# Rotary scores of the cached streams: one fp32r pass over 96 rows in place of an fp32 product over 128

## The chip, the cores and the metric

The kernel runs on one core of a Trainium2 chip. The metric is the device time of one execution in microseconds (us), as the median of several runs. In the views of the profile, PE is TensorE (matrix products and transposes, with PEld for its weight loads), DVE is VectorE, ACT is ScalarE, POOL is GpSimd and SP is SyncE, which here only issues DMAs. TensorE writes into PSUM, the accumulator memory; the others read it from there into SBUF, the working memory of 128 partitions.

## The reference

Two trunk layers of a streaming encoder run on a prompt (512 frames) and on 8 streams of 16 new frames, each stream with 512 cached frames. A layer is a feed-forward block, a block of mixers side by side (latent attention "MLA" with 8 heads, mLSTM, HGRN2), and a second feed-forward block. The change touches the latent attention of the streams:

```python
s = einsum('bqhc,bkc->bhqk', q_lat, ckv) + einsum('bqhr,bkr->bhqk', q_pe, kpe)   # 128 latent + 32 rotary
s = s.astype(float32) * MLA_SCALE                       # streams: every key is allowed
p = softmax(s, axis=-1)
o_lat = einsum('bhqk,bkc->bqhc', p, ckv)
# streams: ckv = concat(cache_ckv (8, 512, 128), new 16 rows), kpe = concat(cache_kpe (8, 512, 32), new 16 rows)
```

A stream's 8 heads by 16 frames are 128 queries, so its scores are a 128 x 528 matrix: a latent part over 128 rows and a rotary part over 32. The softmax and the output do not depend on the order of the keys, as long as scores and values use the same order.

## The kernel before

Each engine has its own program, written out by hand, and they meet in semaphores. An `event(name, n)` is a semaphore that counts n steps per layer; `wait_ge(*e.nth(l, k))` waits for step k of layer l. Within an engine the order of the code is the order of the work, and an instruction that waits holds up everything behind it. DMA loads are issued from SP's or POOL's queue.

A layer's `mla(l)` has two stages.

**The prompt's attention** runs over n = 0 to 31 (NT = 32), which is head h = n // 4 and query tile i = n % 4. PE makes the scores two steps ahead (`attend_scores`, L1144), DVE takes the maximum (`maximum`, L2656), ACT the exponential (`probabilities`, L1891), PE transposes (`attend_transpose`, L1157), ACT copies the result out of PSUM (`transposed`, L1901), and for every odd head PE makes the outputs of two heads (`attend_values`, L1166). Between these steps each engine has other work at fixed n: the query and key products of later heads (`head_queries`, L1114; it waits, for its second half, for `ql_sb`, the copies that ACT makes in `latent_queries`, L1885), the gates of the mLSTM (DVE and ACT), and on POOL the taps of a convolution (`tap_of`, L3195). `latent_queries` puts the streams' latent queries of one head into QLAT and the rotary ones into rows 0 to 31 of QPE. DVE zeroes rows 32 to 127 of KPT (which lies in GB) at n = 2 (L2800, L2801), and POOL rows 32 to 127 of QPE behind its taps (L3164, L3165). After these POOL issues the two stores of the gate maxima out of GB. ACT's first copy of stream keys waits for the arrival of those stores.

**The stream loop** runs over b = 0 to 7, pipelined by two. For a stream PE transposes the 512 cached latent rows (`stream_keys`, L1203, L1209) and the 512 rotary rows (`stream_rope_keys`, L1211, L1213), ACT copies both out of PSUM (`stream_keys`, L1998) into CT and into rows 0 to 31 of KPT, and PE makes the scores (`stream_scores`, L1216): the latent product (L1223), the rotary product (L1224) and the same two for the 16 new keys (L1225, L1226). DVE takes the maximum (L2807), ACT the exponential, DVE normalises, PE transposes (L1236, L1237), ACT copies, and PE makes the outputs (`stream_values`, L1239, L1245). Between these, PE and DVE run the HGRN2 mixer's levels: `level_step` on PE (L1111) makes products, and `level` on DVE (L2675, L2696) merges them under a mask; the next `level_step` waits for the merge. DVE's `scaled` (L2865, L2866) prepares a later level from what POOL (`distances`) and ACT (`decays`) made.

The cache rows come in by POOL's DMAs (`cache`, L3114), one latent and one rotary load per stream, with a semaphore per buffer (CBUF = 4). Streams 0 and 1 are loaded in the projection stage into a part of Y; streams 2 and 3 after the last output product of the prompt and two memsets; stream b from 4 on after the values of stream b − 4.

The products of fp32 data take more passes through the array than those of the type fp32r, in which a value keeps only its high part. The feed-forward blocks already split values into a high and a low fp32r part and add three products (L734 to L736).

## Time and profile before

| what | us |
|---|---|
| median of 3 runs (lowest, highest) | 2607.68 (2606.23, 2608.65) |
| the profiled execution | 2606.66 |
| its span in the profile | 2604.8 |
| PE busy | 2562.2 (98%) |
| PEld busy | 2446.6 (94%) |
| DVE busy | 1644.5 (63%) |
| ACT busy | 1137.5 (44%) |
| POOL busy | 532.3 (20%) |

Most of the span is feed-forward and projection products. The mixers' stages lie from about 605 to 805 us (layer 0) and from 1890 to 2090 us (layer 1). A row of a timeline gives start, length, engine, line, operation, output and input tiles and shapes, a count where several instructions are merged, and in brackets how long the engine stood idle before it and what released it. A matmul's length includes its latency, so the distance between the starts of two rows says how long the first one holds the engine. ACT's work is all issued by one helper, so its rows have line L1536 and are told apart by their tiles; KPT's rows are those of tile `gb`.

### The profile page before, as it was taken

To read this page: it belongs to the slowest core of one execution; us is meant where nothing else is said; L and a number is where in the kernel's file an instruction comes from. 1 tells how busy PE (TensorE), PEld (TensorE's weight loads), DVE (VectorE), ACT (ScalarE), POOL (GpSimd) and SP (SyncE) were. 2 spreads that over 40 slices of the span, in tenths; PEclk is the share of its full clock that TensorE was granted. 3 is DMA by queue.
4 is the path that set the end of the run, shared out by engine and by line. 5 is a ranking of instruction groups with operands and counts; after the bars stand their busy time and mean duration, and the time that the engine had idled before them with its cause. 6 is when DMAs were issued, how large, how long until landed. Compare 5 with 4: busy or idle time off the path is not lost.

```text
span 2604.8 us, 44565 instructions
## 1 busy us (share of the span) xinstructions
PE 2562.2 (98%) x17872; PEld 2446.6 (94%) x17872; DVE 1644.5 (63%) x2566; ACT 1137.5 (44%) x1922; POOL 532.3 (20%) x440
## 2 busy tenths in 40 slices
PE   8999999999999999999999999999999999999998
PEld 8999999996689999999999999999956899999998
DVE  5666575646466866657577574765564757757473
ACT  5343344424654534334454342553165535434253
POOL 0010112103754101011210110121066441101011
PEclk9999999999999999999999999999999999999999
DMA  3322324220025122232313222334100161322231
GB/s 116 91 81 81 97 65 113 73 59 11 20 54 100 49 82 81 84 95 71 108 33 96 83 71 76 89 89 105 27 11 30 46 130 34 97 81 71 85 85 59
DMA packets 369794, 190.73 MB, mean 73 GB/s; under 512 B 38541, under 2 KB 365536, under 8 KB 369630
## 3 DMA queue, kind: packets, MB, share of 16 engines
q1 hardware_dynamic: 365248, 177.89, 25.3%
q0 software_dynamic: 4000, 10.47, 1.8%
q8 instruction: 108, 1.77, 0.3%
q14 instruction: 56, 0.46, 0.1%
q10 hardware_dynamic: 382, 0.14, 0.0%
HBM read 182.53 MB, written 5.93 MB: 72 GB/s over the span
## 4 chain that ended last, share of the span: by engine, by line
PE 90%; DVE 4%; POOL 2%; ACT 2%; issue 1%; DMA 1%; SPq 0%; DVEq 0%; POOLq 0%; ACTq 0%
PE ps L734 27%; PE ps L735 27%; PE ps L736 27%; PE ps L1111 2%; POOL misc L3201 1%; POOL qkc L3204 1%; PE ps L1122 1%; PE ps L1223 1%; DVE at L2696 1%; PE ps L1224 1%; PE ps L1154 0%; PE ps L1245 0%; PE ps L1173 0%; ACT css L1536 0%; PE ps L1236 0%
## 5 line engine op out<-in xcount | busy, mean ns | idle before, releaser
L734 PE MATMUL ps<-xh,w 128*128 128x320 f32 x1920 | 595.3, 310 | 2.8 <-DVE css L2961 2.8
L736 PE MATMUL ps<-xh,w 128*128 128x320 f32 x1920 | 593.5, 309 | 0.0
L735 PE MATMUL ps<-xl,w 128*128 128x320 f32 x1920 | 593.4, 309 | 0.0
L1536 ACT ACTIVATE w<-raw 128x512 fp32r<-128x512 f32 (+3 forms) x372 | 315.8, 861 | 484.2 <-PE ps L736 466.2
L3058 POOL TENSOR_TENSOR hl<-ub,hh 128x640 fp32r<-128x640 f32 x88 | 174.1, 1978 | 1448.4 <-ACT hh L1536 1381.3
L734 PE MATMUL ps<-hh,w 128*128 128x320 f32 x1408 | 438.1, 311 | 3.3 <-DVE ub L2352 1.2
L735 PE MATMUL ps<-hl,w 128*128 128x320 f32 x1408 | 435.2, 309 | 0.0
L736 PE MATMUL ps<-hh,w 128*128 128x320 f32 x1408 | 435.2, 309 | 0.0
L734 PEld LDWEIGHTS ps<-xh,w 128*128 128x128 f32 x1920 | 360.4, 188 | 4.9 <-DVE css L2961 3.2
L735 PEld LDWEIGHTS ps<-xl,w 128*128 128x128 f32 x1920 | 360.4, 188 | 0.3
L736 PEld LDWEIGHTS ps<-xh,w 128*128 128x128 f32 x1920 | 360.4, 188 | 0.0
L734 PEld LDWEIGHTS ps<-hh,w 128*128 128x128 f32 x1408 | 264.3, 188 | 8.4 <-issue 8.0
L735 PE MATMUL ps<-tc,w 128*128 128x320 f32 x864 | 267.1, 309 | 0.0
L734 PE MATMUL ps<-tc,w 128*128 128x320 f32 x864 | 267.1, 309 | 0.0
L736 PE MATMUL ps<-tc,w 128*128 128x320 f32 x864 | 267.1, 309 | 0.0
L735 PEld LDWEIGHTS ps<-hl,w 128*128 128x128 f32 x1408 | 264.3, 188 | 0.5
L736 PEld LDWEIGHTS ps<-hh,w 128*128 128x128 f32 x1408 | 264.3, 188 | 0.0
L2363 DVE TENSOR_TENSOR y<-ps,y 128x640 f32<-128x640 f32 x83 | 68.3, 823 | 262.0 <-PE ps L736 262.0
L2227 DVE TENSOR_TENSOR w<-raw,w 128x512 fp32r<-128x512 f32 (+1 forms) x216 | 180.1, 861 | 3.9 <-ACT w L1536 3.9
L734 PEld LDWEIGHTS ps<-tc,w 128*128 128x128 f32 x864 | 162.2, 188 | 0.0
L736 PEld LDWEIGHTS ps<-tc,w 128*128 128x128 f32 x864 | 162.2, 188 | 0.0
L735 PEld LDWEIGHTS ps<-tc,w 128*128 128x128 f32 x864 | 162.2, 188 | 0.0
(418 smaller groups left out, 4671.2 us busy)
## 6 DMA issues: line engine op xcount, KB each, us to landing
raw<-in_w_ffn_in_dram SPq DMA_DIRECT2D x176, 512.0 KB
raw<-in_w_ffn_out_dram SPq DMA_DIRECT2D x192, 192.0 KB
raw<-in_w_in_dram SPq DMA_DIRECT2D x38, 512.0 KB
raw<-in_w_ffn_out_dram SPq DMA_DIRECT2D x64, 128.0 KB
wraw<-in_w_out_dram SPq DMA_DIRECT2D x8, 512.0 KB
raw<-in_w_out_dram SPq DMA_DIRECT2D x8, 512.0 KB
out_dram<-xio SPq DMA_DIRECT2D x5, 512.0 KB
xin<-in_x_prompt_dram SPq DMA_DIRECT2D x4, 512.0 KB, 7.6
```

Source lines behind the costliest of these rows:

```text
L734: pe.matmul(out, wh, xh, start=first, stop=False, skip_group_check=loose)
L735: pe.matmul(out, wh, xl, start=False, stop=False, skip_group_check=loose)
L736: return pe.matmul(out, wl, xh, start=False, stop=last, skip_group_check=loose)
L1111: mm = pe.matmul(PS[:, 6 + h % 2, at:at + w], k_, q_, start=True, stop=True)
L1122: mm = pe.matmul(PS[:, half, 0:HALF], WUQ[:, c, h, :], CQ[:, c, half * HALF:(half + 1) * HALF], start=c == 0, stop=c == 1)
L1223: pe.matmul(PS[:, 4, :], ql, CT[:, b % 2, :], start=True, stop=False)
L1224: pe.matmul(PS[:, 4, :], qp, KPT[:, b % 2, 0:PAST], start=False, stop=True)
L1536: return nc.scalar.activation(out, in_, func, **kw)
L2227: V.tensor_tensor(lo, group_raw(n, q % 2), hi.bitcast(F32), ALU.subtract)\
L2363: ins = V.tensor_tensor(y, ps, y, ALU.add) if add else V.tensor_copy(y, ps)
L2696: ins = V.copy_predicated(out, mask, new)
L3058: G.tensor_tensor(HL[:, k, :], UB[:, j, :], HH[:, k, :].bitcast(F32), ALU.subtract).then_inc(hl_ready.sem, 1)
```

## The change

The rotary queries and keys of the streams are split in three blocks of 32 rows, in fp32r: queries high, low, high (QPR), keys high, high, low (KPR). One product over 96 rows then gives high x high + low x high + high x low. The zeroed rows and their memsets go. To get three copies of the keys in three blocks of partitions, the rotary cache rows are loaded three times side by side (CK tiles of 96 columns) and transposed at once; ACT copies all 96 rows, and DVE subtracts the high part in the third block (`stream_keys_low`). The queries are split inside the attention: ACT copies at n = 22 and n = 29 (`rope_high`), DVE subtractions at n = 24 and n = 31 (`rope_low`). The new keys are copied by ACT at n = 23 and split by DVE at n = 25. In `stream_scores` the latent products of old and new keys come first, then a wait for the low keys, then the rotary ones. The cache rows are read so that a partition gets four neighbouring rows. Stream 1's three rotary loads move behind the end of the prompt's attention, and stream 3's loads wait for stream 1's transposes.

```diff
-CACHE_TURNS = [len(range(c, NSEQ, CBUF)) for c in range(CBUF)]
+CACHE_LOADS = [4] * NSEQ
+CACHE_TURNS = [sum(CACHE_LOADS[c::CBUF]) for c in range(CBUF)]
...
+    KPR = tile(s_w, "kpr", [3 * ROPE, 2, T], F32R)
...
+    QPR = tile(s_q, "qpr", [3 * ROPE, NSEQ, H, TS], F32R)
...
-    CK = [y45[:, 1024 + b * P:1024 + (b + 1) * P].rearrange("p (k c) -> p k c", k=4) for b in range(2)] + \
-        [CK2[:, b, :, :] for b in range(2)]
+    CK = [Y[:, 0:4, TP:TP + 3 * ROPE]] + [CK3[:, b % 2, :, :] for b in range(1, NSEQ)]
...
         def stream_rope_keys(l, b):
+            if b:
+                pe.wait_ge(*klo_sb.nth(l, b - 1))
             for k in range(4):
-                mm = pe.transpose(PS[0:ROPE, 1, k * P:(k + 1) * P], CK[b % CBUF][:, k, :], IDENT[:, :])
+                cut = slice(k * P, (k + 1) * P)
+                mm = pe.transpose(PS[0:3 * ROPE, 1, cut], CK[b][:, k, :], IDENT[:, :])
...
             pe.matmul(PS[:, 4, :], ql, CT[:, b % 2, :], start=True, stop=False)
-            pe.matmul(PS[:, 4, :], qp, KPT[:, b % 2, 0:PAST], start=False, stop=True)
             pe.matmul(PS[:, 5, 0:TS], ql, CKVT[:, TP + b * TS:TP + (b + 1) * TS], start=True, stop=False)
-            pe.matmul(PS[:, 5, 0:TS], qn, KN[:, b * TS:(b + 1) * TS], start=False, stop=True)\
+            if b == 0:
+                pe.wait_ge(*qlo_sb.nth(l, 1))
+            pe.wait_ge(*klo_sb.nth(l, b))
+            pe.matmul(PS[:, 4, :], qp, KPR[:, b % 2, 0:PAST], start=False, stop=True)
+            pe.matmul(PS[:, 5, 0:TS], qp, KN[:, b * TS:(b + 1) * TS], start=False, stop=True)\
                 .then_inc(ss_ps.sem, 1)
...
+            def rope_high(n, heads):
+                act.wait_ge(*ql_sb.nth(l, heads.stop - 1))
+                for row in (0, 2 * ROPE):
+                    ins = run(QPR[row:row + ROPE, :, heads, :], QPE[:, :, heads, :], ACT.Copy)
+                ins.then_inc(qh_sb.sem, 1)
+
+            def new_keys():
+                for e in range(3):
+                    ins = run(KN[e * ROPE:(e + 1) * ROPE, :], KPER[NOPE:QK, TP:T], ACT.Copy)
+                ins.then_inc(kn_sb.sem, 1)
...
+                if n == 22:
+                    rope_high(0, slice(0, 6))
+                if n == 23:
+                    new_keys()
                 if n == NT - 3:
+                    rope_high(1, slice(6, H))
                     gate_columns()
...
+            def stream_keys_low(b):
+                dve.wait_ge(*ct_sb.nth(l, b))
+                low = slice(2 * ROPE, 3 * ROPE)
+                V.tensor_tensor(KPR[low, b % 2, 0:PAST], PS[low, 1, :], KPR[low, b % 2, 0:PAST].bitcast(F32), ALU.subtract)\
+                    .then_inc(klo_sb.sem, 1)
+
+            def rope_low(n, heads):
+                dve.wait_ge(*qh_sb.nth(l, 2 * n))
+                V.tensor_tensor(QPR[ROPE:2 * ROPE, :, heads, :], QPE[:, :, heads, :], QPR[0:ROPE, :, heads, :].bitcast(F32),
+                                ALU.subtract).then_inc(qlo_sb.sem, 1)
...
-                if n == 2:
-                    V.memset(KPT[ROPE:64, :, 0:PAST], 0.0)
-                    V.memset(KPT[64:P, :, 0:PAST], 0.0)
+                if n == 24:
+                    rope_low(0, slice(0, 6))
+                if n == 25:
+                    dve.wait_ge(*kn_sb.nth(l, 0))
+                    V.tensor_tensor(KN[2 * ROPE:, :], KPER[NOPE:QK, TP:T], KN[2 * ROPE:, :].bitcast(F32), ALU.subtract)
+                if n == NT - 1:
+                    rope_low(1, slice(6, H))
             inverse_sums(H // 2 - 1)
+            stream_keys_low(0)
             pair_output(H // 2 - 1)
...
             for b in range(NSEQ):
+                if b + 2 < NSEQ:
+                    stream_keys_low(b + 2)
                 level(m)
...
-                load(cache_in[c], CC[c], A["cache_ckv"][l, b].rearrange("(k p) c -> p k c", p=P))
-                load(cache_in[c], CK[c], A["cache_kpe"][l, b].rearrange("(k p) c -> p k c", p=P))
+                load(cache_in[c], CC[c], A["cache_ckv"][l, b].rearrange("(p k) c -> p k c", p=P))
+                keys = A["cache_kpe"][l, b].rearrange("(p k) c -> p k c", p=P)
+                for e in range(3 if b != 1 else 0):
+                    load(cache_in[c], CK[b][:, :, e * ROPE:(e + 1) * ROPE], keys)
...
-            G.memset(QPE[ROPE:64, :, :, :], 0.0).then_inc(pn_zero.sem, 1)
-            G.memset(QPE[64:P, :, :, :], 0.0).then_inc(pn_zero.sem, 1)
...
             G.memset(PNEW[:, :, :], 0.0).then_inc(pn_zero.sem, 1)
+            for e in range(3):
+                load(cache_in[1], CK[1][:, :, e * ROPE:(e + 1) * ROPE],
+                     A["cache_kpe"][l, 1].rearrange("(p k) c -> p k c", p=P))
             cache(2)
             for b in range(3, NSEQ):
+                if b == 3:
+                    pool.wait_ge(*ct_ps.nth(l, 1))
```

## Rows read from the trace of the kernel before

**Rows 1.** The page's second section: granted TensorE clock in 40 slices, tenths.
```profile
PEclk9999999999999999999999999999999999999999
```
**Rows 2.** Waits of PE over the whole span: total us, times, longest.
```profile
PE ps L1163 <- ACT pb L1536: 8.7, 16, 1.2
...
PE ps L1111 <- DVE at L2696: 1.7, 8, 0.2
```
**Rows 3.** Timeline of PE: stream 2's scores in layer 0, until the next mixing step.
```profile
713.09 1.02 PE L1223 MATMUL ps<-ct,qlat 128*128 128x512 f32 x2
713.95 1.02 PE L1224 MATMUL ps<-gb,qpe 128*128 128x512 f32 x2
714.80 0.29 PE L1225 MATMUL ps<-ckvt,qlat 128*128 128x16 f32 x2
715.03 0.39 PE L1226 MATMUL ps<-kn,qpe 32*128 32x16 f32 x2
715.35 0.33 PE L1111 MATMUL ps<-qk 64*128 64x64 f32 x2
```
**Rows 4.** By line: fp32r passes of 512 columns, ns min/median/max, first and last start.
```profile
L866 PE MATMUL ps<-spin x22: 380/382/793, 1.2 to 1984.2; 128*128 128x512 f32 x22
...
L1333 PE MATMUL ps<-maskr,idr x10: 474/479/504, 763.9 to 2068.2; 128*128 128x512 f32 x10
```
**Rows 5.** POOL's cache loads and those who wait: timelines, and the loads' landing.
```profile
701.87 0.78 POOL L3090 DMA_DIRECT2D cc<-in_cache_ckv_dram  x1
...
DMA to landing us min/median/max: 2.8/2.9/3.1
...
704.31 0.66 PE L1209 MATMUL ps<-ident,y 128*128 128x128 f32 x4
...
733.49 0.76 POOL L3090 DMA_DIRECT2D cc<-in_cache_ckv_dram  x1 [2.55 <-PE ps L1245]
...
739.40 0.60 PE L1209 MATMUL ps<-ident,cc 128*128 128x128 f32 x4
...
1984.89 1.13 PE L1223 MATMUL ps<-ct,qlat 128*128 128x512 f32 x2 [0.27 <-ACT kn L1536]
```
**Rows 6.** Timelines of ACT and DVE in the attention of layer 0, n = 22 to 25.
```profile
681.09 0.59 ACT L1536 ACTIVATE kt<-ps 64x512 f32<-64x512 f32 x1
...
682.42 0.47 ACT L1536 ACTIVATE pb<-ps,mx 128x256 f32<-128x256 f32 x1
...
683.03 0.25 ACT L1536 ACTIVATE qpe<-ps 32x128 f32<-32x128 f32 x1
...
681.43 0.42 DVE L2661 TENSOR_REDUCE mx<-ps 128x1 f32<-128x256 f32 x1
```
**Rows 7.** Timeline of PE in the same stretch: head 7's queries, a later transpose.
```profile
684.13 1.24 PE L1122 MATMUL ps<-cq,wuq 128*128 128x320 f32 x4
...
688.02 0.65 PE L1163 MATMUL ps<-ident,pb 128*128 128x128 f32 x4 [1.24 <-ACT pb L1536]
```
**Rows 8.** Timelines: instructions from which the added ones are sized.
```profile
754.02 1.26 ACT L1536 ACTIVATE kdf<-kdf 128x1280 f32<-128x1280 f32 x1
...
718.20 0.82 DVE L2865 TENSOR_TENSOR qk<-y,dd 128x640 f32<-128x640 f32 x1
```
**Rows 9.** Timelines: a DVE pair of one shape twice, and a tap on POOL.
```profile
653.12 2.01 DVE L2743 TENSOR_TENSOR ub<-mpv,r 4x512 f32<-4x512 f32 x2
...
655.77 0.87 DVE L2748 TENSOR_TENSOR gb<-g,ge 4x512 f32<-4x512 f32 x2
...
685.39 1.56 POOL L3201 TENSOR_SCALAR misc<-extp,par 128x512 f32<-128x512 f32 x1
```
**Rows 10.** Timelines around DVE's memsets: PE's scores, the fourth maximum's first instruction.
```profile
623.95 1.02 PE L1154 MATMUL ps<-kt,qt 128*128 128x512 f32 x2
...
625.50 0.11 DVE L2660 MEMSET ps<- 64x64 f32 x1
```
**Rows 11.** Timeline of DVE: the maximum of stream 2, and its idle time before.
```profile
715.45 0.71 DVE L2807 TENSOR_REDUCE mx<-ps 128x1 f32<-128x528 f32 x1 [1.47 <-PE ps L1226]
```

## What the change will do to the time

> **What bounds the kernel now.** I read the page's engine rows first: PE (TensorE) is busy for 98% of the span (in the table above), and its granted clock is at the full level, 2.4 GHz, in every slice [rows 1]. So only what shortens or delays PE counts. The change touches one stage of each of the two layers: the prompt's attention (about 618 to 700 us in layer 0, the same at 1901 to 1983 us in layer 1) and the loop over eight streams behind it (700 to 757 us, and 1984 to 2041 us). I then asked who makes PE wait. In the stream loop nearly nobody: the mixing steps wait for DVE 1.7 us in all, 0.2 at most [rows 2]. There PE's own work is the clock. In the attention it is different: PE waits there for the probabilities that ACT computes, up to 1.24 us at a time [rows 7], and the order scores (PE), maximum (DVE), exponential (ACT), transpose (PE) sets the pace. An instruction put into ACT's or DVE's queue there can land on PE's path. The last view is the timeline around each place that the diff edits.
>
> **Gain: the rotary product.** For stream 2 the latent product starts at 713.09, the rotary one at 713.95, the new latent keys at 714.80, the new rotary keys at 715.03, and the next mixing step at 715.35 [rows 3]. So the rotary product holds PE 0.85 us (two records) and the new rotary keys 0.32, which includes the drain before rows of another height: 1.17 us. After the change the rotary product is one fp32r pass of 512 columns. The two fp32 records take 1.02 together, the second 0.43 behind the first, so one lasts 0.59 and 0.16 of it is latency. Two rows show an fp32r pass of this size: the warm-up product with 382 ns, which holds PE 0.22, and the mask product with 479, which is 0.32 [rows 4]. Now the pass stands behind a wait for DVE, so its weights can't be loaded early, and I take the upper price, 0.32. The new keys keep some 0.25 of load and drain. That leaves 0.57 of 1.17: **0.6 us saved per stream**, with bounds of 0.42 (0.15 more for the wait and the taller rows) and 0.72 (the lower price, and 0.2 for the new keys). The four transposes of rotary keys get 96 columns of weights instead of 32. The 128-wide ones beside them pass at the same pace, so that is nothing, at most 0.1 with the same sign as the bound above. Stream 0's saving is lost in the wait below; seven streams give 4.2 us per layer (2.9 to 5.0).
>
> **Cost: the cache rows of stream 1.** Their three rotary loads are now issued by POOL behind the last attention product and two memsets. Those are the instructions in front of the first DMA at 701.87 [rows 5]. An issue holds POOL 0.75, so the third starts at 701.87 + 1.5 = 703.4, and such a load lands 2.9 us after its issue [rows 5]: 706.3. PE transposes stream 1 at 704.31 now [rows 5]. It sits behind the first mixing step and would be ready 0.6 sooner, at 703.7, so PE stands still for some 2.6 us and restarts **2.0 us later** than before. Queued behind this wait are the second mixing step, stream 0's transpose and all later scores, and nothing later is late for its own reason, so all of it is paid (bounds 1.6 and 2.5, from the spread of the landing and a slower third load). In layer 1 the latent product of stream 0 began about 0.4 later than in layer 0, because ACT's copy waited for the store of the gates (PE idle 0.27 and a slower first record) [rows 5]. That store is issued after two memsets which the change removes, so this wait goes, and in layer 1 only 1.6 is lost. The later streams' loads are four issues in place of two. Stream 6 is the tight one: POOL issues it at 733.49 and PE wants it at 739.40 [rows 5], 5.9 later, or 5.3 with the saving; four issues need 2.26 to the last start and 2.9 to its landing, 5.2. I put it at nothing.
>
> **Cost: splitting the queries inside the attention.** ACT gets two copies of 32x768 behind the key copy at 681.09, before the exponential at 682.42 [rows 6]. That key copy of 512 takes 0.59 and a copy of 1280 takes 1.26 [rows 8], each about 0.1 less when another follows; 768 costs 0.73, two cost 1.46, ending at 683.1. DVE is the real trouble: its subtraction of 32x768 is queued ahead of the maximum that now runs at 681.43 [rows 6], and it waits for those copies. At 0.82 for 640 elements [rows 8] it holds DVE 0.87 and ends at 684.1. Then come the maximum (0.57), the exponential (0.45, to 685.2), three copies of new keys at 0.22 (685.8), and the query rows of head 6, which now end at 683.28 [rows 6] and would end at 686.2. PE's product for head 7 waits for exactly these: 684.13 now [rows 7], 686.3 then, **2.2 us late**, and the scores, maximum and exponential behind it move with it, since the idle 1.24 before 688.02 [rows 7] is that same chain and no slack. On top there is POOL. A pair of DVE instructions of 4x512 took 2.01 us in one place and 0.87 in the next, both beside POOL's convolution taps [rows 9]. So a DVE subtraction can be held by a POOL instruction, whose length is 1.56 [rows 9], and POOL runs taps without a pause here. The query and key subtractions both stand in it. I add 0.4, bounds 0 and 1.3. The second part of the queries, 32x256, sits in idle time of ACT near 696 us; it delays the gate columns by 0.6, which PE takes up only 0.8 later. In sum **+2.6 per layer** (bounds 1.2, if part of it falls into PE's waits, and 3.5).
>
> The Trainium skill, page SBUF — State Buffer, section "Who interferes with whom", says that a DVE instruction with two SBUF inputs and a GpSimd instruction that reads SBUF shut each other out for a whole instruction. The two durations above agree. By that rule in full the layer-0 delay would be 3.4 and the layer-1 delay 2.4, which gives almost my sum.
>
> **Small terms.** DVE loses its two memsets behind the third maximum. The fourth maximum starts at 625.50, right behind them and the rotation, though PE's scores, started at 623.95, are done at 625.0 [rows 10]: −0.4 per layer (bounds 0 and −0.6). DVE gains one subtraction of 32x512 per stream, about 0.65 by its 640-element row [rows 8]. It stands ahead of a mixing step and a maximum, and before that maximum DVE is idle 1.47 us [rows 11], which covers it. In streams 6 and 7, where the mixing copies are longer, some 0.1 each shows: +0.2 per layer (0 to 1.0). The fuller ACT copy of keys has the same 512 elements per row: nothing. The earlier cache issue in the projections lies in POOL's idle time: nothing.
>
> **The sum.** Layer 0: −4.2 + 2.0 + 2.6 − 0.4 + 0.2 = +0.2. Layer 1: −4.2 + 1.6 + 2.6 − 0.4 + 0.2 = −0.2. Together 0.0 us on a profiled execution of 2606.66 (span 2604.8). The median of the runs is 2607.68, so the forecast is **2607.7 us**: what the single pass wins is given back at two places. A measurement of this kernel can tell about 0.2% (5.2 us) from no change; that is the bound of my three chances.
>
> **Rivals.** (1) The attention hides its additions, because PE's waits for ACT are wide there (16 waits, 8.7 us in both layers [rows 2]). Then +2.6 becomes about +0.5 in each layer, and with 0.72 saved per stream (−0.85 per layer more) the time is 2607.7 − 4.2 − 1.7 = 2601.8. Against it stands that DVE's maximum is ordered behind the subtraction. Chance 0.15. (2) The other side: the idle PE in front of stream 1 costs it its clock. The clock stayed at 2.4 GHz everywhere, but no wait of PE in this stage exceeds 1.24 us [rows 7], and the new one has 2.6. If the clock fell to 1.2 GHz, the work from 704.31 until the latent product of stream 2, about 8 us at full speed after the saving, would run at half speed for a part; half of it costs 4 us per layer: 2607.7 + 8 = 2615.7. It decides from the moment that the granted clock of that window is under 1. Chance 0.1. The Trainium skill, page TensorE: Matmul & The Clock Gate, section "HAM oscillation — how this bites in real kernels", says that a wait between bursts can put the engine back to the half clock; nothing in this trace shows it. (3) The single pass is none in effect: it holds PE 0.43 like one fp32 record, and the wait for DVE adds 0.15. Then a stream saves 1.17 − 0.43 − 0.15 − 0.25 = 0.34, which is 0.26 less, and the time is 2607.7 + 14 × 0.26 = 2611.3. Chance 0.1, with a third of it past the bound once POOL's holds are added. The forecast itself has 0.65.
>
> **How the numbers follow.** The forecast's own range is ±4: 14 streams by 0.15 (2.1), two layers by 0.9 for the attention and 0.5 for the landing, not all of one sign. It lies inside the bound, and 0.05 of it leaks past on either side by those terms. The range reaches to 2602.0 and 2613.0, which takes in rival 3 and part of rival 1. Faster: 0.12 of rival 1 and 0.03, 0.15. Slower: 0.1 of rival 2 and 0.06 of the others, 0.16. Same: 0.69.
>
> **What the profile after would show.** The rotary product as one record near 382 to 479 ns, and about 1.65 us from latent product to mixing step in place of 2.26. PE idle for 2.5 to 3 us before stream 1's transposes, released by a DMA. In the attention PE's product for head 7 later by 2 to 3 us, DVE idle before the query subtraction and ACT idle before the exponential behind it. Wrong would be: no wait before stream 1 (the loads land sooner), a delay under 1 us at head 7, or a granted clock under 1 behind the wait.

## The result and the profile after

The changed kernel takes 2614.97 us in the median of 7 executions (2609.99 to 2619.74), before on the same chip 2606.78 of 7 (2606.18 to 2608.65): a ratio of 1.0029 with a 95% interval of [1.002, 1.0038]. It is slower by 8.2 us; I had forecast no change and given 2602 to 2613. The profiled execution of the changed kernel is its fastest, 2609.99 us with a span of 2608.2. The six others lie 3 to 10 us above it.

The page of the profile after:

```profile
span 2608.2 us, 44591 instructions
...
PE 2556.6 (98%) x17840; PEld 2445.1 (94%) x17840; DVE 1656.7 (64%) x2584; ACT 1147.2 (44%) x1934; POOL 552.0 (21%) x468
...
PEclk9999999999999999999999999999999999999999
```

PE is as busy as before, 98%, and the slices' granted clock looks full, for a slice is 65 us. The mean granted clock that belongs to each execution says more: 0.999 for the profiled execution of before, 0.996 for the profiled one after, 0.992 to 0.995 for the six others after. A whole span of 2608 at 0.995 has lost 13 us of PE's full clock, if PE was busy all that time. The waits of PE in the whole span (us in total, times, longest), which answer to [rows 2]:

```profile
PE ps L1172 <- ACT pb L1548: 11.0, 16, 1.5
PE ps L1218 <- DMA ck<-in_cache_kpe_dram: 4.3, 2, 2.2
PE ps L1131 <- ACT qpe L1548: 3.7, 4, 1.2
...
PE ps L1120 <- DVE at L2734: 3.2, 12, 0.4
```

New is the wait for the DMA of CK (2.2 in each layer). The query product's waits for ACT rose from 1.1 in all, 0.5 at most, to 3.7 and 1.2. The waits for the probabilities rose from 8.7 to 11.0, their longest from 1.2 to 1.5, and the mixing steps' waits for DVE from 1.7 to 3.2. Line numbers have moved: L1122 is L1131 now (query product), L1154 is L1163 (scores), L1163 is L1172 (transposes), L1209 is L1218 and L1213 is L1225 (a stream's transposes), L1223 is L1234 (latent product) and L1225 is L1235 (the same for the new keys), L1111 is L1120 (mixing steps). The rotary products are L1239 and L1240.

**The attention, layer 0.** PE's timeline, which answers to [rows 7]:

```profile
682.66 0.91 PE L1163 MATMUL ps<-kt,qt 128*128 128x384 f32 x2
685.11 0.44 PE L1172 MATMUL ps<-ident,pb 128*128 128x128 f32 x2 [1.53 <-ACT pb L1548]
686.75 2.47 PE L1131 MATMUL ps<-cq,wuq 128*128 128x320 f32 x4 [1.20 <-ACT qpe L1548]
689.01 1.91 PE L1163 MATMUL ps<-kt,qt 128*128 128x512 f32 x2
...
692.82 0.66 PE L1172 MATMUL ps<-ident,pb 128*128 128x128 f32 x4 [0.82 <-ACT pb L1548]
```

The transposes of n = 25 followed the scores with no wait before. Now PE stands still 1.53 us before them and 1.20 more before the second query product of head 7. The rows behind them are twice as long as before: a query product of four records 2.47 in place of 1.24, the scores of 512 columns 1.91 in place of 1.02. This is the clock. ACT's, DVE's and POOL's timelines of that place say why PE waits, as [rows 6] did before:

```profile
681.20 1.69 ACT L1548 ACTIVATE qpr<-qpe 32x768 fp32r<-32x768 f32 x2
...
684.49 0.47 ACT L1548 ACTIVATE pb<-ps,mx 128x256 f32<-128x256 f32 x1 [1.30 <-DVE mx L2688]
...
685.08 0.94 ACT L1548 ACTIVATE kpr<-kper 32x128 fp32r<-32x128 f32 x3
...
686.34 0.27 ACT L1548 ACTIVATE qpe<-ps 32x128 f32<-32x128 f32 x1
```

```profile
682.92 0.95 DVE L2699 TENSOR_TENSOR qpr<-qpe,qpr 32x768 fp32r<-32x768 f32 x1 [3.56 <-ACT qpr L1548]
...
684.03 0.42 DVE L2688 TENSOR_REDUCE mx<-ps 128x1 f32<-128x256 f32 x1
...
686.06 0.75 DVE L2841 TENSOR_TENSOR kpr<-kper,kpr 32x128 fp32r<-32x128 f32 x1 [1.36 <-ACT kpr L1548]
```

```profile
681.33 1.56 POOL L3251 TENSOR_SCALAR misc<-extp,par 128x512 f32<-128x512 f32 x1
682.87 1.40 POOL L3252 TENSOR_SCALAR misc<-exts,par 128x128 f32<-128x128 f32 x1
```

ACT's two copies run until 682.89, then DVE's subtraction of 32x768 takes 0.95, then come the maximum and the exponential (684.49, was 682.42), the three new keys, and the query rows of head 6, which end at 686.61 (were 683.28). The three copies of new keys are 0.94 together, 0.31 each. DVE's subtraction of only 128 elements takes 0.75, begun 0.08 behind the start of a POOL instruction of 1.56; in a place without one it took 0.28 (in r4_fix_both, below). POOL's own tap of 128 elements at 682.87 lasts 1.40, where its others last 0.60.

**The granted clock.** Windows of PE (length, busy, records, granted clock, DMA share, GB/s) at both places, first layer 0's attention, then layer 1's first streams; before had 1.00 throughout both stages:

```profile
684.00:686.00 2.00, 0.44 (x2) 0.92 0.00 0
686.00:688.00 2.00, 1.25 (x3) 0.50 0.00 0
688.00:690.00 2.00, 2.00 (x5) 0.50 0.03 8
...
692.00:694.00 2.00, 1.18 (x14) 0.88 0.21 64
1990.00:1992.00 2.00, 0.58 (x12) 1.00 0.27 86
1992.00:1994.00 2.00, 1.25 (x7) 0.74 0.60 176
1994.00:1996.00 2.00, 2.00 (x17) 0.50 0.21 66
...
2000.00:2002.00 2.00, 2.00 (x26) 1.00 0.00 0
```

In layer 0 the clock falls to 0.50, that is 1.2 GHz, at 685.7: behind the wait of 1.53 and 0.44 of work, and just inside the second wait. It comes back at about 692.5, 6.8 us later. In layer 1 PE had the same two waits in its attention and the clock stayed at 2.4 GHz. There it fell behind the other new wait, again for 6.8 us:

```profile
1992.75 0.95 PE L1218 MATMUL ps<-ident,y 128*128 128x128 f32 x4 [2.16 <-DMA ck<-in_cache_kpe_dram]
...
1994.48 1.97 PE L1120 MATMUL ps<-qk 64*128 64x64 f32 x16
```

The wait of 2.16 before stream 1's transposes is in both layers, at 710.63 in layer 0, where the clock stayed full. So in this execution each layer lost its clock at one of two places. POOL's timeline shows what the wait in layer 0 is for; [rows 5] has the same place before:

```profile
704.78 1.16 POOL L3217 MEMSET at<- 128x1280 f32 x1 [9.09 <-PE ps L1182]
705.88 0.94 POOL L3218 MEMSET pnew<- 128x1024 f32 x1
706.78 2.27 POOL L3136 DMA_DIRECT2D ck<-in_cache_kpe_dram  x3
```

**The gain.** Stream 3 of the changed kernel, answering to [rows 3]; the first row is the mixing step behind stream 2's scores:

```profile
720.50 1.11 PE L1120 MATMUL ps<-qk 64*128 64x64 f32 x16 [0.39 <-DVE at L2734]
...
725.37 1.02 PE L1234 MATMUL ps<-ct,qlat 128*128 128x512 f32 x2
726.23 0.29 PE L1235 MATMUL ps<-ckvt,qlat 128*128 128x16 f32 x2
726.37 0.48 PE L1239 MATMUL ps<-kpr,qpr 96*128 96x512 f32 x1
726.69 0.17 PE L1240 MATMUL ps<-kpr,qpr 96*128 96x16 f32 x1
726.79 1.11 PE L1120 MATMUL ps<-qk 64*128 64x64 f32 x16
```

From latent product to mixing step it is 1.42 us, where before needed 2.26. The rotary pass holds PE 0.32, the new keys 0.10. Not every stream keeps all of it: stream 2 needed 1.89 (718.61 to 720.50), for its mixing step waited 0.39 for DVE, and stream 1 needed 1.60.

**The ledger.** Distances between the same steps in both traces give each part. I compare each layer with its own start, since layer 1 began its attention 0.51 late.

| part, us | layer 0 | layer 1 |
|---|---|---|
| memsets of DVE gone (up to n = 24) | −0.47 | −0.22 |
| the attention's chain behind head 7 | +5.3, of it 2.1 half clock | +3.2 |
| from there to stream 1's restart (stream 0's gain is lost in its wait, the store's wait is gone) | +1.5 | +1.0 |
| seven streams | −4.7 | −1.7, of it 3.1 half clock |
| sum | +1.6 | +2.2 |

The 2.1 is 5.3 less the 3.2 of the same steps in layer 1 at full clock; the 3.1 is what the steps between 1992.75 and 2000.05 took over their length in before, with the score's saving of 0.84 added. Between the layers 1.1 us were won back (0.8 of it is a wait of PE for POOL that is gone; none of the change's steps lies there), and the last 15 us of the kernel, where both have two stretches of half clock, cost some 0.7 more. 1.6 − 1.1 + 2.2 + 0.7 is the 3.4 by which the span grew. Without the two falls the layers would be −0.5 and −0.9.

The kernel before is not free of half clock either. The same windows of its trace near its end:

```profile
2590.00:2592.00 2.00, 2.00 (x20) 0.99 0.03 8
2592.00:2594.00 2.00, 2.00 (x11) 0.50 0.00 0
2594.00:2596.00 2.00, 2.00 (x15) 0.66 0.00 0
```

From 2591.9 the clock was at 0.50 for 3.4 us, with PE busy throughout, in a run of products of one column and then transposes; from 2602.1 it was at 0.50 again, with PE idle. At the kernel's start PE waited 2.08 us (before 9.16) and kept its clock. The slices of [rows 1] show none of this.

### The profile page after: what moved, and what is told of

Same layout as the page of the kernel before. It is cut to its first block, busy times and chain, and to the rows that moved or that the text cites. A ratio compares the mean times of both kernels' runs of the same rounds, so it can differ in the third digit from the quotient of the medians.

```text
span 2608.2 us, 44591 instructions
## 1 busy us (share of the span) xinstructions
PE 2556.6 (98%) x17840; PEld 2445.1 (94%) x17840; DVE 1656.7 (64%) x2584; ACT 1147.2 (44%) x1934; POOL 552.0 (21%) x468
## 4 chain that ended last, share of the span: by engine, by line
PE 90%; DVE 5%; ACT 2%; issue 2%; DMA 0%; SPq 0%; POOL 0%; DVEq 0%; ACTq 0%; POOLq 0%
PE ps L743 27%; PE ps L744 27%; PE ps L745 27%; PE ps L1120 1%; PE ps L1131 1%; PE ps L1163 1%; DVE at L2734 1%; DVE mx L2688 0%; ACT pb L1548 0%; PE ps L1182 0%; PE ps L1172 0%; ACT css L1548 0%; PE ps L1234 0%; PE ps L1259 0%; DVE wt L2924 0%
```

## The experiments

Theory C (the clock): the change's waits cost their length, and behind each of them PE can fall to 1.2 GHz, in some executions at one place and in some at another; this costs the greater part of the 8.2 us. Theory W (the waits): the waits alone cost, and the clock is a bystander. Each kernel was timed against before on the same chip.

| kernel (executions) | median us (lowest, highest) | before us | ratio, 95% interval | median of the mean granted clock (before: 0.998 to 0.999) |
|---|---|---|---|---|
| r1_late_keys (11) | 2611.88 (2610.55, 2615.94) | 2606.98 | 1.0021 [1.0012, 1.003] | 0.997 |
| r2_split_alone (6) | 2615.73 (2612.87, 2616.52) | 2606.98 | 1.0029 [1.0017, 1.0041] | 0.998 |
| r3_fill (11) | 2605.84 (2604.21, 2609.55) | 2606.98 | 0.9995 [0.9986, 1.0004] | 0.999 |
| r4_fix_both (11) | 2605.86 (2600.64, 2608.45) | 2606.98 | 0.9994 [0.9985, 1.0003] | 0.996 |
| r5_attention_moved (12) | 2607.71 (2601.55, 2611.58) | 2608.16 | 0.9996 [0.9987, 1.0004] | 0.996 |
| r6_loads_first (11) | 2605.11 (2601.83, 2612.15) | 2608.16 | 0.999 [0.9982, 0.9999] | 0.997 |
| r7_both_moved (5) | 2597.17 (2594.51, 2601.06) | 2608.16 | 0.9962 [0.9949, 0.9975] | 0.998 |
| r8_low_behind_mask (9) | 2600.95 (2599.82, 2609.93) | 2608.16 | 0.9979 [0.997, 0.9989] | 0.998 |
| r9_both_and_fill (5) | 2597.32 (2595.62, 2598.02) | 2606.75 | 0.9962 [0.9948, 0.9976] | 0.998 |
| r10_fill_attention (11) | 2609.0 (2607.62, 2615.6) | 2606.75 | 1.0017 [1.0008, 1.0026] | 0.997 |
| r11_fill_stream (11) | 2607.88 (2605.52, 2608.62) | 2606.75 | 1.0002 [0.9993, 1.0011] | 0.998 |
| r12_fp32_product (11) | 2605.29 (2603.4, 2607.0) | 2606.75 | 0.9993 [0.9984, 1.0002] | 0.999 |

**One part of the change alone, on before.** First the late load:

```diff
-                load(cache_in[c], CK[c], A["cache_kpe"][l, b]...)
+                if b != 1:
+                    load(cache_in[c], CK[c], A["cache_kpe"][l, b]...)
...
             cache(2)
+            load(cache_in[1], CK[1], A["cache_kpe"][l, 1]...)
```

> Before, with one move: stream 1's rotary rows are loaded behind stream 2's rows, so that they land about 2 us too late, as in the changed kernel. Nothing else of the change is in it. Both theories expect PE idle for some 2 us before stream 1's transposes in each layer. Theory W (the waits alone cost): 2606.8 + 2 x 2.0 = 2610.8 us, the granted clock at 2.4 GHz behind the wait. Theory C (the clock falls behind such a wait, in some executions): the same 4.0, and up to 3.1 more per layer, the price of the fall in layer 1 of the changed kernel's trace: 2612 to 2617, with a mean granted clock under that of before.

Measured: PE waited 1.54 in layer 0 and 1.03 in layer 1, less than I had meant, and the median is 4.9 above before. 2.6 of it are the waits. The windows of the trace have the rest (columns as above):

```profile
704.00:706.00 2.00, 0.46 (x7) 1.00 0.56 125
706.00:708.00 2.00, 2.00 (x24) 0.81 0.33 127
708.00:710.00 2.00, 2.00 (x9) 0.50 0.00 0
1990.00:1992.00 2.00, 1.14 (x17) 1.00 0.61 174
1992.00:1994.00 2.00, 1.83 (x22) 1.00 0.52 150
```

In layer 0 the clock went down to 1.2 GHz 1.6 us behind the end of the wait of 1.54, for 3.4 us; in layer 1, behind 1.03, it stayed. This is before's own code with one load moved. Of 11 executions eight lie at 2610.6 to 2612.4 with a mean clock of 0.997 or 0.998, three at 2614.2 to 2615.9 with 0.996 or 0.997. Two groups alone prove nothing: before's own 28 executions lie at 2604.5 to 2607.0 with 0.999 or 1.000 (15 of them) and at 2607.8 to 2609.0 with 0.998. What theory W does not give is the fall in the trace, and clocks under those of before.

Then the attention's additions:

```diff
+                if n == 22:
+                    rope_high(0, slice(0, 6))      # ACT: QPE rows 32:64 and 96:128 <- QPE rows 0:32
+                if n == 23:
+                    new_keys()
...
+                if n == 24:
+                    rope_low(0, slice(0, 6))       # DVE: QPE rows 64:96
```

> Before, with the attention's additions alone: the two copies of 32x768 and of 32x256, the three copies of new keys and the three subtractions at the same n as in the changed kernel (written into rows of QPE that the product multiplies with zero), and without the two POOL memsets of QPE. The product stays the fp32 one over 128 rows. Theory W: PE's chain behind head 7 later by 3.2 us per layer (as in layer 1 of the changed kernel's trace, where the clock held): 2606.8 + 6.4 - 0.4 = 2612.8, clock full. Theory C: up to 2.1 per layer more, the price of the fall in layer 0: 2613 to 2617, clock under that of before. The rival that the attention hides the additions: 2607.

Measured 2615.73, in two groups again: 2612.9 and 2613.1 with a clock of 0.999, and four executions of 2615.6 to 2616.5 with 0.997 or 0.998. The first group is on the point of theory W (2612.8), the second in the range of theory C; the 3 us between them are more than the 2.0 between the middles of before's groups. PE's timeline (line numbers here are three above those of before) shows the same waits and the same doubled record as the changed kernel, in layer 0 as here and again in layer 1 (1.54 and 1.07, then 1.85 for the four records):

```profile
685.58 0.44 PE L1166 MATMUL ps<-ident,pb 128*128 128x128 f32 x2 [1.54 <-ACT pb L1539]
687.08 2.47 PE L1125 MATMUL ps<-cq,wuq 128*128 128x320 f32 x4 [1.07 <-ACT qpe L1539]
```

So the additions are not hidden; they alone cost 6 us, and the clock some 3 more in four of six executions.

**The waits kept, PE kept busy in them.** A warm-up product writes to a bank of PSUM that nothing needs at that time and holds PE 0.22.

```diff
                 if i == 1 and h + 1 < H:
+                    if n == 25:
+                        spin(PS[:, 7, :], 5)
                     head_queries(l, h + 1, 1)
...
+                if n == 24:
+                    pe.wait_ge(*kt_sb.nth(l, H - 1))
+                    spin(PS[:, 7, :], 6)
                 if n + 1 < NT:
                     attend_transpose(l, n + 1)
...
             level_step(l, 0)
+            spin(PS[:, 2, :], 9)
             stream_keys(l, 1)
```

> The changed kernel, with PE kept busy in its three new waits: six warm-up products of 512 columns before the transposes of n = 25, five before the second query product of head 7, nine before stream 1's transposes (0.22 us each, about the length of the waits: 1.53, 1.20 and 2.16). No wait is shortened and nothing else changes. Theory W: nothing changes, 2615. Theory C: the granted clock is at 2.4 GHz in both stages in every execution, and the time is that of the changed kernel's profiled execution less its two falls (2.1 and 3.1) and the 0.7 at the end of the kernel: 2604, eleven under the changed kernel.

Measured 2605.84: 9.1 us under the changed kernel, though no step of the change is moved and PE has more to do. In its trace head 7's second query product of layer 0 starts at 686.78, where the changed kernel's did at 686.75. Every window of both stages has a granted clock of 1.00; half clock comes only from 2588 on, near the end of the kernel, where before has it too. This rules theory W out. It is the clearest of the runs. With only one of the places filled:

> The changed kernel with only the two attention waits filled (six and five warm-up products). r3_fill, with all three waits filled, took 9.1 us off the changed kernel's median. Theory C divides this by the price of a fall at each place: 2.1 per layer here and 3.1 behind stream 1, so 2615.0 - 9.1 x 0.4 = 2611.3. Theory W: 2615.

> The changed kernel with only stream 1's wait filled (nine warm-up products). Theory C: the larger part of the 9.1 us, 2615.0 - 9.1 x 0.6 = 2609.5. Theory W: 2615.

Measured 2609.0 and 2607.88, 6.0 and 7.1 under the changed kernel, both more than my shares of 3.7 and 5.5; together they give 9.1, not 13. The prices of falls don't add, and I can't say why from these runs. In r11's trace the attention of both layers had a fall, each of 3.4 us where the changed kernel's was of 6.8; in r10's only layer 1 had one behind stream 1's wait, of 6.8. r10 is in two groups: seven executions of 2607.6 to 2609.5 (clock 0.997 or 0.998), four of 2614.6 to 2615.6 (0.994). With stream 1's wait left open, about one execution in three lost some 6 us more.

**The waits taken away.** The attention's steps move to idle times of ACT and DVE:

```diff
-                if n == 22:
-                    rope_high(0, slice(0, 6))
-                if n == 23:
-                    new_keys()
+                if n == 25:
+                    rope_high(slice(0, 6), (0,))
+                if n == 26:
+                    rope_high(slice(0, 6), (2 * ROPE,), last=True)
+                if n == 28:
+                    new_keys()
...
-                if n == 24:
+                if n == 30:
                     rope_low(0, slice(0, 6))
...
```

The second part of the queries (heads 6 and 7) moves back in the same way. The three loads of stream 1 go, in r4, from POOL to SP; in r6 and r7 they are one DMA of POOL ahead of its memsets, and DVE's wait for the second memset moves behind its first mask:

```diff
+            load(cache_in[1], CK[1].rearrange("p k (e c) -> p k e c", e=3),
+                 A["cache_kpe"][l, 1]....unsqueeze(2).broadcast_to([P, 4, 3, ROPE]))
...
             G.memset(ATB[:, AT_HALF:2 * AT_HALF, :], 0.0)...
             G.memset(PNEW[:, :, :], 0.0)...
-            for e in range(3):
-                load(cache_in[1], CK[1][:, :, e * ROPE:(e + 1) * ROPE], ...)
```

> The changed kernel with both waits taken away. The rotary loads of stream 1 are issued by SP's idle queue as soon as the last output product of the attention is done, not behind POOL's memsets. The copies and subtractions of queries and new keys move to idle times of ACT and DVE: ACT's high copies of heads 0 to 5 at n = 25 and 26, new keys at 28, heads 6 and 7 at 30; DVE's subtractions at n = 30, 31 and behind the last inverse sums. Both theories expect what the single pass and the dropped memsets win, read off the changed trace: 0.5 for the memsets, 0.9 for stream 0, 0.84 for stream 1, 4.0 for the other six, per layer, and 0.4 for the store in layer 1: 2606.8 - 12.9 + about 0.6 that the moved steps still cost = 2594.5. If the time is above 2603, the loss lies in neither wait but in the product, its loads or the subtractions of the stream loop.

Measured 2605.86, eleven above the expectation. The loads from SP did not come in time: PE waited 0.8 in layer 0 and 3.09 in layer 1, where they ran beside POOL's loads for stream 2 (168 GB/s in that window). PE's timeline in layer 1 (line numbers here are seven above those of the changed kernel):

```profile
1986.01 0.63 PE L1225 MATMUL ps<-ident,y 128*128 128x128 f32 x4 [3.09 <-issue]
...
1988.72 1.12 PE L1257 MATMUL ps<-ident,sp 128*128 128x128 f32 x4
```

The transposes of P (the second row) take 1.12 in place of 0.66: half clock again, for 13.6 us. Another stretch of half clock, of 6.8 us, lay in the first 20 us of the kernel, in which no step differs from before; it began 1.8 us behind the end of a wait of 2.32 for the prompt's rows. The fastest executions were 2600.6 and 2601.2. The edit failed at its aim, so this run shows only one more fall behind a wait. A longer wait doesn't mean a longer fall: r5 and r8, below, spent 20 us at half clock behind waits of 2.19 and 1.05.

> The changed kernel with the attention's copies and subtractions moved to idle times of ACT and DVE (as in r4_fix_both), and stream 1's rotary loads as in the changed kernel, behind the memsets. Theory W (the waits alone): the attention's +3.2 per layer goes: 2615.0 - 6.2 = 2608.8. Theory C (the clock's falls behind the waits as well): up to 2.1 per layer more, while the fall behind stream 1's wait stays: 2605 to 2609, with a mean granted clock above the changed kernel's 0.995. The trace should show PE's product for head 7 within 0.2 of its place relative to the scores of n = 25, and stream 1's wait of 2.2 as it was.

> The changed kernel with stream 1's three copies of the rotary rows as one DMA whose source is read three times, issued by POOL ahead of its two memsets; the attention stays as changed. The wait of 2.2 should shrink to under 0.5 in both layers. Theory W: 2615.0 - 4.4 = 2610.6. Theory C: up to 3.1 per layer more: 2605 to 2610, with the granted clock behind stream 0 at 2.4 GHz, and the fall in the attention still there in some executions.

> Both of these at once. r4_fix_both took the attention's waits away, but its loads from SP's queue still left PE idle 0.8 us in layer 0 and 3.1 in layer 1, with the clock at half behind the latter. Here no wait over 1.3 us should be left in either stage, so both theories give what the single pass wins: 2594 to 2598. If the time stays near 2606 with the clock under 0.998, the clock falls without such a wait, and theory C has the wrong cause.

Measured: r5 2607.71, r6 2605.11, r7 2597.17. r5 doesn't tell the theories apart (2608.8 against 2605 to 2609); r6 is 5.5 under theory W's 2610.6 and at the lower end of theory C's 2605 to 2610. In r5 the attention's waits are as in before and the clock there is full; the wait of 2.2 at stream 1 stands, and the profiled execution, its slowest, fell to half clock in both layers, 0.9 us before the end of the wait in layer 0 and 0.8 us behind it in layer 1, for about 7 and 20 us. In r6 the wait at stream 1 is 1.0, the attention as changed, with half clock for some 3 us in it in layer 1. r7 has neither:

```profile
PE ps L1172 <- ACT pb L1548: 8.9, 14, 1.2
...
PE ps L1120 <- DVE at L2738: 3.2, 12, 0.4
...
PE ps L1218 <- DMA ck<-in_cache_kpe_dram: 1.9, 2, 1.0
```

Its profiled execution, the fastest of five, has a span of 2592.6, 12.2 under that of before's profile, and 1.00 in every window of both stages. Its median is 11.0 under that of before on the same chip (a ratio of 0.9962), so it beats both kernels. This is what the single pass and the dropped memsets win. The edit for the loads was not as good as I said (1.0 of wait left, not under 0.5), since the DMA of three times the elements landed 4.2 us after its issue in layer 0, where the changed kernel's loads took 2.3 to 3.2.

> r7_both_moved with four warm-up products in what is left of stream 1's wait (1.0 us) and five in the wait of 1.2 before the transposes of n = 27, which the kernel before has too. Theory C: the executions of r7_both_moved that took 2596 to 2601 with a clock of 0.997 to 0.999 lost it behind these waits, so the median falls from 2597.2 to that of the fastest, 2594.5 to 2595.5. If the falls that are left lie at the kernel's end alone, the median stays at 2597.

Measured 2597.32: nothing won. The trace has its only half clock from 2580 on, at the kernel's end. What spreads r7 from 2594.5 to 2601 is not, or not often, behind these waits; the second branch of the expectation holds.

**DVE's subtraction in the stream loop.** On top of r7:

```diff
-                if b + 2 < NSEQ:
-                    stream_keys_low(b + 2)
                 level(m)
+                if b + 2 < NSEQ:
+                    stream_keys_low(b + 2)
```

> r7_both_moved with DVE's subtraction for the keys of stream b + 2 behind the masked copy of the level in place of ahead of it. In the changed kernel PE waits 1.6 us per layer for these copies, 0.4 at most, where before waited 0.9. If the subtraction's place is the cause, that falls back to 0.9 or under, and the time is 1 to 2 us under that of r7_both_moved. If the rotary product then waits for its low rows, the same is lost there and nothing changes.

Measured 2600.95, slower than r7. PE's waits for the masked copies fell from 1.6 to 0.9 per layer, as said, but the rotary product now waits 1.1 and 1.6 per layer for its low rows. And in the profiled execution, r8's slowest, layer 0 ran at half clock for 20 us behind this wait:

```profile
704.72 0.66 PE L1218 MATMUL ps<-ident,y 128*128 128x128 f32 x4 [1.05 <-DMA ck<-in_cache_kpe_dram]
...
706.03 1.97 PE L1120 MATMUL ps<-qk 64*128 64x64 f32 x16
```

r7 had the same wait of 0.98 at this place and kept its clock. So one wait of 1.0 can be enough, and need not be.

**The product by itself.** On top of r7:

```diff
+            qp = qp.bitcast(F32)
-            pe.matmul(PS[:, 4, :], qp, KPR[:, b % 2, 0:PAST], start=False, stop=True)
+            pe.matmul(PS[:, 4, :], qp, KPR[:, b % 2, 0:PAST].bitcast(F32), start=False, stop=True)
```

> r7_both_moved with the rotary products of the same 96 rows as fp32 products, everything else the same. It prices the single pass by itself. The fp32 rotary product held PE 0.85 in the trace of before and the fp32r pass holds 0.32 in that of the changed kernel, the new keys 0.22 and 0.10, so 0.65 per stream and 16 streams make 10.4: 2597.2 + 10.4 = 2607.6, which would be before's time again. If the saving came from elsewhere, the time stays near 2597.

Measured 2605.29, 8.1 over r7, or 9.5 if each is taken against before on its own chip. Stream 2 in its trace:

```profile
714.09 1.11 PE L1240 MATMUL ps<-kpr,qpr 96*128 96x512 f32 x2
715.04 0.29 PE L1241 MATMUL ps<-kpr,qpr 96*128 96x16 f32 x2
715.26 1.11 PE L1120 MATMUL ps<-qk 64*128 64x64 f32 x16
```

The product holds PE 0.95 and the new keys 0.22, 1.17 in all; the single pass needs 0.42. That is 0.75 per stream and 12.0 in all. Given back are 1.4 (the waits for masked copies are 0.9 per layer in place of 1.6) and 1.3 (the longer score of stream 0 hides the load: a wait of 0.4 and 0.2 in place of 1.0 and 0.9); 9.3 remain, near the 8.1 and 9.5 of the medians and the 8.9 between the fastest executions. The saving is the product's.

## Why the prediction was wrong

**The step that failed** is the first sentence of my reading, that the clock is at 2.4 GHz in every slice and so only what shortens or delays PE counts, carried over to the changed kernel. I worked out two new idle stretches of PE myself, and priced both at their length. The reading was wrong for before too: in the last 15 us of its trace the clock is at 0.50 twice. The behaviour stood as rival 2, with a chance of 0.1 and only at stream 1's wait. That its 2615.7 is within 0.8 of the median is luck: it adds 8 us at one place to a sum of 0.0, where the runs put some 10 us at two places on a sum of −1.8 (below). The runs put it at both places: r1 and r2 show it with one part of the change on before's own code, and r3 takes 9.1 us away by feeding PE in the waits. Against it I had put that no wait of PE in this stage exceeds 1.24 us and the clock holds. That is no evidence on longer waits, and the change's are 2.16, and 1.53 with 1.20 close behind it. The page TensorE: Matmul & The Clock Gate of the Trainium skill, section "HAM oscillation — how this bites in real kernels", says that waits between bursts of products put the engine back to the half clock. The traces agree in kind (0.50 behind 2.16 us of idle, and behind 1.53 of idle and 0.44 of work); its case has longer waits than any of these, and the fall in before's trace with PE busy is no case of it.

**The terms**, against the traces at full clock:
- Rotary saving: 0.6 per stream, measured 0.84. The fp32 product held what I said. I took 0.25 for the new keys behind it; they hold 0.10, and as an fp32 product of the same 96 rows, in r12, 0.22, where the 32 rows behind 128 had held 0.32: 0.10 of the 0.32 went with the change of height, 0.12 with fp32r. The other 0.09 of the 0.84 lies in the new latent keys, which hold 0.14 in place of 0.23 now that the pass of 96 rows follows them. The upper bound of 0.72 was passed.
- The stream loop's subtraction: +0.2 per layer, measured +0.75 (waits for the masked copies 1.7 to 3.2 in both layers). I had looked at the maximum behind it and called it covered, and sized the copies' wait too small. Within its bounds.
- Seven streams with both: −4.0, measured −4.7 and, less the fall, −4.8.
- Stream 1's loads: idle 2.6, measured 2.16; each landed 2.3 us after the third issue, not 2.9. The net +2.0 and +1.6 became +1.5 and +1.0. The mechanism and its place were right.
- The attention: +2.6, measured +3.2 at full clock and 6 us for both layers in r2. The chain came as written (copies, subtraction, maximum, exponential, new keys, query rows, head 7). The new keys were 0.31 each and not 0.22, the copies 0.84 and not 0.73. POOL held DVE at one of the two subtractions: that of new keys took 0.75, and 0.28 without POOL beside it; POOL's own tap was stretched from 0.60 to 1.40 in turn. The rule of the page SBUF — State Buffer of the Trainium skill, section "Who interferes with whom", agrees with this in part: they did hold each other, but not for a whole instruction, since the subtraction ended 0.73 before the POOL instruction beside it, and in r2 the same subtraction took 0.28 inside a POOL instruction of 1.56.
- DVE's memsets: −0.4, measured −0.5 and −0.2. Later streams' loads: no wait, as said.
- The clock: put at nothing, measured 2.1 and 3.1 in the profiled execution, which is the fastest, and some 10 in the median.

The two layers without their falls are −0.5 and −0.9 where I had +0.2 and −0.2. With the −1.1 between them and the +0.7 at the end that makes 2606.66 − 1.8 = 2604.9 us: inside my range and inside the bound for no change. The median of 2614.97 is 10.1 above it; the mean clock of 0.995 in place of 0.999 is worth 10.4 of 2608 us, to within its rounding. r2's two fastest executions (0.1 and 0.3 from the sum without falls) and r3 show the same. Rival 1 (the attention hides it) is refuted by r2, rival 3 (the pass is none) by r12.

**What stays open.** Whether a given wait costs the clock differs from execution to execution and from layer to layer: of the two equal waits of 2.16 in the profiled execution one did and one didn't, and the time at 1.2 GHz was about 3.4 us (r1, r6), 6.8 (the changed kernel), 13.6 (r4) or 20.5 (r5, r8). Nor is a wait the only thing that goes before a fall, as before's at 2591.9 shows. Nor do the prices of r10 and r11 add up to r3's. I tried no run that sets the length of one wait in steps. For a single execution I can't say where the clock was lost, since only one execution of each kernel has a trace; that the others lost it behind the same waits is inferred from their mean clock and from r3.

## What to carry to other kernels

A new wait of TensorE has two prices, its length and the clock behind it, and the second can be as large: here single waits of 1.05 to 3.1 us went with 3 to 20 us at 1.2 GHz in some executions, and with none in others. Look at the mean granted clock of each execution beside its time, not only at the slices of one profile, and price a new wait by its range over executions. Where a wait can't be removed at once, fill it with warm-up products of its length (r3: −9.1 us, with nothing else changed); better, move the small copies and subtractions behind the chain that TensorE waits for, and loads ahead of memsets (r7: 11 us under before, where the changed kernel was 8 over it).

## What the runs showed of the hardware

- Granted clock 0.50 for 3.4 to 20.5 us, begun behind (in r5 also in) a single idle stretch of 1.05 (r8), 1.54 (r1), 2.16 (the changed kernel), 2.19 (r5) or 3.09 us (r4), with TensorE busy before it and after it; and 1.00 behind others of 0.98 (r7), 1.03 (r1), 1.24 and 2.08 (before) and 2.16 (the changed kernel).
- Granted clock 0.50 for 3.4 us with no idle stretch: before's trace from 2591.9, TensorE busy for 2.00 of every 2.00 us, with products of one column and transposes.
- A product of the same height as the one before it held PE for less: as fp32, the new keys' product of 16 columns held it 0.22 with 96 rows behind 96 (r12) and 0.32 with 32 rows behind 128 (before); as fp32r with 96 behind 96 it was 0.10.
- One DMA with a source that is read three times held POOL for about 1.05 us, from its start to the next instruction, where three DMAs held it for 2.25, and its rows landed early enough for a wait of 1.0 in place of 2.2, ahead of 2.1 us of memsets.
- Three loads from SP's queue held that queue for 2.02 us in layer 0 and for 3.32 in layer 1, where POOL's loads ran beside them, and PE waited 0.8 and 3.09 for them.
